# Recurrent gate products in two row halves, and the last chunks one round later

## What is computed

```python
q, k, v, rx, rg, ga, gb = split(modulate(x) @ w_in)      # 16 rounds of two tiles, and v
attn = chunk_band_attention(q, k, v)                     # 8 heads of 64
xc = causal_conv4(rx)
r  = sigmoid(xc_blocks @ wa + ba)                        # 8 blocks of 64 x 64
ig = sigmoid(xc_blocks @ wx + bx)                        # 8 blocks of 64 x 64
a  = exp(-8 * r * softplus(-lam))
u  = sqrt(1 - a*a) * (ig * xc)
h  = linear_scan(h[t] = a[t] * h[t-1] + u[t])
rnn = h * gelu(rg)
x  = x + gate * ((sigmoid(ga) * (attn @ wA) + sigmoid(gb) * (rnn @ wB)) @ w_out)
x  = x + gate * conv_ffn(modulate(x))
y  = rmsnorm(x)
```

## Time and profile before

| what | value |
|---|---|
| time, median of 3 runs | 2693.74 us (2689.85 to 2702.45) |
| span of the profiled execution | 2692.3 us |
| TensorE busy | 2645.6 us, 98% |
| VectorE, ScalarE, GpSimd busy | 1750.8, 1362.9, 628.2 us |
| mean granted TensorE clock | 0.992 |
| DMA | 423.07 MB, mean 157 GB/s |

### The profile page before, as it was taken

The page is one execution under the profiler, slowest core; times in us unless marked ns, Lnnn a source line. Parts: engine busy times, 40 slices in busy tenths (PEclk is TensorE's granted clock), DMA queues, the critical chain, the costliest instruction groups (busy, mean ns, idle before and its releaser), DMA issues.

```text
span 2692.3 us, 50625 instructions
## 1 busy us (share of the span) xinstructions
PE 2645.6 (98%) x18664; PEld 1771.5 (66%) x18664; DVE 1750.8 (65%) x3367; ACT 1362.9 (51%) x2666; POOL 628.2 (23%) x698
## 2 busy tenths in 40 slices
PE   7999999999999999999999999999999999999998
PEld 2466666666668888557996666666666666666665
DVE  4966464655646666776778788888888875242433
ACT  4967474755656666113556555565555653121211
POOL 2600000000008889000000254433344311101000
PEclk9999999999999999999999999999999999999999
DMA  8621322031294442556552354445545438567572
GB/s 281 200 74 66 135 78 105 25 109 71 93 231 95 112 156 105 183 210 202 143 142 69 126 181 166 171 168 189 181 159 179 165 120 325 212 233 262 210 249 106
DMA packets 238419, 423.07 MB, mean 157 GB/s; under 512 B 57816, under 2 KB 162776, under 8 KB 230056
## 3 DMA queue, kind: packets, MB, share of 16 engines
q1 hardware_dynamic: 229400, 412.03, 46.1%
q10 hardware_dynamic: 8848, 8.74, 1.0%
HBM read 283.42 MB, written 139.92 MB: 157 GB/s over the span
## 4 chain that ended last, share of the span: by engine, by line
PE 84%; DVE 5%; ACT 4%; DMA 3%; issue 2%; POOL 1%; SPq 0%; DVEq 0%; ACTq 0%; POOLq 0%
PE ps L2988 57%; PE ps L3240 14%; PE ps L3080 4%; PE ps L3067 3%; PE ps L3056 2%; DMA arena<-in_w_mod_rest 2%; PE ps L2912 1%; ACT arena L1600 1%; PE ps L3094 1%; POOL arena L1140 1%; PE ps L3029 1%; DVE arena L2393 1%; DVE arena L2471 1%; ACT arena L1607 1%; DVE arena L2089 0%
## 5 line engine op out<-in xcount | busy, mean ns | idle before, releaser
L2988 PE MATMUL ps<-arena 128*128 128x352 f16 (+1 forms) x11880 | 1613.1, 297 | 5.1 <-ACT arena L1768 2.1
L2988 PEld LDWEIGHTS ps<-arena 128*128 128x128 f16 x11880 | 1100.6, 97 | 513.1 <-ACT arena L1768 2.5
L3240 PE MATMUL ps<-arena 128*128 128x352 f16 x2772 | 414.9, 310 | 0.5 <-DVE arena L2689 0.5
L3240 PEld LDWEIGHTS ps<-arena 128*128 128x128 f16 x2772 | 264.7, 96 | 150.8 <-issue 1.0
L1197 POOL TENSOR_TENSOR arena<-arena 128x128 f32<-128x128 f32 x44 | 30.6, 695 | 740.4 <-DMA arena<-in_w_down 740.1
L3094 PE MATMUL ps<-arena 128*128 128x424 f16 (+1 forms) x960 | 172.5, 341 | 2.1 <-DVE arena L2471 1.4
L1760 ACT ACTIVATE arena<-ps 128x352 f32<-128x352 f32 x264 | 116.3, 460 | 98.8 <-PE ps L2988 98.8
L1153 POOL CAST arena<-arena 64x512 f16<-64x512 f32 x8 | 4.9, 610 | 689.6 <-DMA arena<-in_cache_kT 689.3
L3080 PE MATMUL ps<-arena 128*128 128x64 f32 (+2 forms) x1200 | 151.0, 272 | 0.5 <-DVE arena L2435 0.5
L1207 POOL TENSOR_TENSOR arena<-arena 128x176 f32<-128x176 f32 (+1 forms) x57 | 56.2, 986 | 398.4 <-DMA arena<-ffn_hidden 398.4
L3080 PEld LDWEIGHTS ps<-arena 128*128 128x128 f32 (+2 forms) x1200 | 144.4, 193 | 3.4 <-issue 2.1
(11 more groups left out here) (239 smaller groups left out, 3587.1 us busy)
## 6 DMA issues: line engine op xcount, KB each, us to landing
hidden_combinations<-arena SPq DMA_DIRECT2D x48, 616.0 KB, 3.2
arena<-hidden_combinations SPq DMA_DIRECT2D x24, 1232.0 KB, 7.8
arena<-in_w_up SPq DMA_DIRECT2D x44, 512.0 KB, 4.9
down_combinations<-arena SPq DMA_DIRECT2D x44, 448.0 KB, 2.8
ffn_hidden<-arena SPq DMA_DIRECT2D x44, 440.0 KB, 3.1
arena<-down_combinations SPq DMA_DIRECT2D x10, 1792.0 KB, 7.8
arena<-down_combinations SPq DMA_DIRECT2D x20, 896.0 KB, 6.9
arena<-ffn_hidden SPq DMA_DIRECT2D x50, 352.0 KB, 3.9
```

Of the source, the lines that this page charges most:

```text
L2988: mm = pe.matmul(out, wt[:, k, wp, :], act_t[:, k, hp], start=(first and k == 0 and n == 0), stop=(last and k == K - 1 and n == 2), skip_g ...
L3240: mm = pe.matmul(ps[:, down_bank(n, k), 0:CF].rearrange("p (w t) -> p w t", w=2), dwt(i)[:, wi, wp, :], dact[i][:, :, bi, hp, :], start=(i ...
```

## The change

1. Gate products in two row halves. The weights of a group shrink from 2 x 128 to 128 columns: rows 0 to 63 hold block 2j of both gates, rows 64 to 127 block 2j + 1 of both, with the gates' columns swapped. A chunk has six matmuls again, but each of 64 rows, alternating between the row halves and between banks 4 and 5. Each bank then holds both gates of one block. Both tanh of gates are halved by partition, and two of the four read one partition half and write the other.
2. gates(j, s) is cut in two: gates (the four tanh) and decays (tanh and exp). In i = 0 a c21 is put between them.
3. Chunk 4 gets its gate product in i = 2 behind c = 2 (was i = 1 behind c = 6), chunk 5 in i = 2 behind c = 4 (was c = 2). The steps of chunks 3 to 5 on ScalarE and VectorE move later accordingly; those of chunk 5 end in round i = 3, and with them q_hi and q_lo (from the end of i = 2), k_hi (behind the first copies) and k_lo (behind p_block(r, 0)).
4. VectorE makes the split of weights 2 of the next round (proj_lo) in i = 2 behind the scan of chunk 4.
5. The sync queue stores gate row 0 of the last round ahead of the weight loads instead of behind them. The recurrent stores keep their places.

```diff
-        gw, gws = bufT[:, 0:2 * P], at_(51560, 4 * P, F16).rearrange("p (s n) -> p s n", s=2)
+        gw, gws = bufT[:, 0:P], at_(51560, 2 * P, F16).rearrange("p (s n) -> p s n", s=2)
...
-            return NS * j + (0, 2, 5, 6)[i]
+            return NS * j + (0, 2, 4, 6)[i]
...
             for r in range(NR):
                 j, i = r // 4, r % 4
+                if r and kind_of(r - 1) == GATES:
+                    gate_row(r - 1, 0)
                 if r + 1 < NR:
                     round_tiles(r + 1)
...
                 if r and kind_of(r - 1) == GATES:
-                    gate_row(r - 1, 0)
                     gate_row(r - 1, 1)
...
             def gates(j, s):
...
-                act.activation(cols, ps[:, 4, 0:w], ACT.Tanh, scale=0.5 * CS, bias=half_bias(0, j)).then_inc(x_act, 1)
-                act.wait_ge(x_gate, 2 * n + 2)
+                act.activation(cols[low], ps[low, 4, 0:w], ACT.Tanh, scale=0.5 * CS, bias=half_bias(0, j)[low])
+                act.activation(cols[high], ps[high, 5, 0:w], ACT.Tanh, scale=0.5 * CS, bias=half_bias(0, j)[high])\
+                    .then_inc(x_act, 1)
                 keep_above_zero(act, x_d2, 3 * (n - 1))
-                act.activation(bufI[s % 2][:, 0:w], ps[:, 5, 0:w], ACT.Tanh, scale=0.5 * CS, bias=half_bias(1, j)).then_inc(x_act, 1)
+                act.activation(bufI[s % 2][low, 0:w], ps[high, 4, 0:w], ACT.Tanh, scale=0.5 * CS,
+                               bias=half_bias(1, j)[high])
+                act.activation(bufI[s % 2][high, 0:w], ps[low, 5, 0:w], ACT.Tanh, scale=0.5 * CS,
+                               bias=half_bias(1, j)[low]).then_inc(x_act, 1)
+
+            def decays(j, s):
...
# ScalarE, the loop over r
-                    for q in range(2 if i == 2 else 0, 3):
+                    for q in range((0, 1, 2, 0)[i], 3):
                         c21(r - 1, q)
-                    if i == 2:
-                        rnn_hi(j, 3)
...
                 if i == 2:
-                    gates(j, 4)
+                    chunk_hi(j, 4)
+                    root(j, 3)
+                    rnn_hi(j, 3)
                 if i == 3:
-                    k_hi(j)
+                    root(j, 5)
+                    q_hi(j)
                 for q in range(3):
                     copy(r, 0, q)
...
                 if i == 2:
-                    root(j, 4)
                     tap(j, 5)
-                    chunk_hi(j, 5)
-                    rnn_hi(j, 4)
+                if i == 3:
+                    k_hi(j)
+                    rnn_hi(j, 5)
...
# VectorE, the loop over r
                 if i == 2:
-                    recur1(j, 4)
-                    recur2(j, 4)
-                    conv(j, 5)
+                    chunk_lo(j, 4)
+                    recur2(j, 3)
+                    rnn_product(j, 3)
+                    rnn_lo(j, 3)
+                if i == 3:
+                    recur2(j, 5)
+                    rnn_product(j, 5)
+                    q_lo(j)
+                for q in range(3):
+                    p_block(r, 0, q)
                 if i == 3:
                     k_lo(j)
-                for q in range(3):
-                    p_block(r, 0, q)
+                    rnn_lo(j, 5)
...
                 if i == 2:
-                    rnn_lo(j, 5)
+                    recur1(j, 5)
...
# TensorE
-                for g in range(2):
-                    for m, (wp, hp) in enumerate(PASSES):
-                        mm = pe.matmul(ps[:, 4 + g, 0:w], gws[:, wp, P * g:P * g + P], xsp[hp][:, 0:w],
+                for m, (wp, hp) in enumerate(PASSES):
+                    for g in range(2):
+                        own = slice(64 * g, 64 * g + 64)
+                        mm = pe.matmul(ps[:, 4 + g, 0:w], gws[own, wp, :], xsp[hp][own, 0:w],
                                        start=(m == 0), stop=(m == 2))
-                    mm.then_inc(x_gate, 1)
-
-            GATE_SLOTS = {(0, 3): 0, (0, 5): 1, (1, 2): 2, (1, 4): 3, (1, 6): 4, (2, 2): 5}
+                        if m == 2:
+                            mm.then_inc(x_gate, 1)
+
+            GATE_SLOTS = {(0, 3): 0, (0, 5): 1, (1, 2): 2, (1, 4): 3, (2, 2): 4, (2, 4): 5}
```

More of the change, by code:

```diff
@@ L750, in _ @@
                         sp.wait_ge(x_d2, 3 * NS * j)
-                    sp.dma_start(gw, a["w_rgate"][j].rearrange("p g m -> p (g m)")).then_inc(gw_loaded, 16)
+                    sp.dma_start(gw, a["w_rgate"][j]).then_inc(gw_loaded, 16)
                 if r and kind_of(r - 1) == GATES:
-                    gate_row(r - 1, 0)
                     gate_row(r - 1, 1)
@@ L1478, in gates @@
                 n, (t0, w) = NS * j + s, chunk(s)
-                act.wait_ge(x_gate, 2 * n + 1)
+                low, high = slice(0, 64), slice(64, 128)
+                act.wait_ge(x_gate, 2 * n + 2)
                 act.wait_ge(x_conv, 3 * n + 3)
                 cols = rowA[:, t0:t0 + w]
-                act.activation(cols, ps[:, 4, 0:w], ACT.Tanh, scale=0.5 * CS, bias=half_bias(0, j)).then_inc(x_act, 1)
-                act.wait_ge(x_gate, 2 * n + 2)
+                act.activation(cols[low], ps[low, 4, 0:w], ACT.Tanh, scale=0.5 * CS, bias=half_bias(0, j)[low])
+                act.activation(cols[high], ps[high, 5, 0:w], ACT.Tanh, scale=0.5 * CS, bias=half_bias(0, j)[high])\
+                    .then_inc(x_act, 1)
                 keep_above_zero(act, x_d2, 3 * (n - 1))
-                act.activation(bufI[s % 2][:, 0:w], ps[:, 5, 0:w], ACT.Tanh, scale=0.5 * CS, bias=half_bias(1, j)).then_inc(x_act, 1)
+                act.activation(bufI[s % 2][low, 0:w], ps[high, 4, 0:w], ACT.Tanh, scale=0.5 * CS,
[3 more added lines that the diff above has]
+            def decays(j, s):
+                n, (t0, w) = NS * j + s, chunk(s)
+                cols = rowA[:, t0:t0 + w]
                 act.wait_ge(x_act, 4 * n + 1)
@@ L1546, in _ @@
                     gates(j, 2)
+                    decays(j, 2)
                     tap(j, 3)
                 if i == 2:
-                    gates(j, 5)
+                    chunk_hi(j, 5)
+                    gates(j, 4)
+                    decays(j, 4)
                 if r + 1 < NR:
@@ L1556, in _ @@
                     chunk_hi(j, 3)
+                if i == 2:
+                    root(j, 4)
                 for q in range(3):
@@ L1562, in _ @@
                     gates(j, 0)
+                    decays(j, 0)
                     chunk_hi(j, 1)
@@ L1566, in _ @@
                 if i == 2:
-                    root(j, 5)
+                    rnn_hi(j, 4)
                 if r + 1 < NR:
@@ L1576, in _ @@
                     gates(j, 3)
+                    decays(j, 3)
                     tap(j, 4)
                 if i == 2:
-                    rnn_hi(j, 5)
+                    gates(j, 5)
+                    decays(j, 5)
                 if r + 1 < NR:
@@ L1583, in _ @@
                     gates(j, 1)
-                if i == 1:
-                    root(j, 3)
-                    chunk_hi(j, 4)
+                    c21(r, 0)
+                    decays(j, 1)
                 if i == 1:
@@ L2331, in _ @@
                 if i == 2:
-                    chunk_lo(j, 5)
-                    rnn_product(j, 4)
-                    rnn_lo(j, 4)
+                    conv(j, 5)
                 if i == 0:
@@ L2345, in _ @@
                 if i == 2:
-                    recur1(j, 5)
+                    chunk_lo(j, 5)
+                    recur1(j, 4)
                 if r + 1 < NR:
                     for c in range(3):
+                        if c == 2 and i == 2:
+                            recur2(j, 4)
+                            rnn_product(j, 4)
                         proj_lo(r + 1, c)
@@ L2357, in _ @@
                     rnn_product(j, 2)
-                if i == 2:
-                    recur2(j, 5)
-                    rnn_product(j, 5)
                 if r + 1 < NR:
+                    if i == 2:
+                        rnn_lo(j, 4)
                     proj_lo(r + 1, 3)
@@ L2380, in _ @@
                     recur1(j, 1)
-                if i == 1:
-                    recur2(j, 3)
-                    rnn_product(j, 3)
-                    rnn_lo(j, 3)
-                if i == 2:
-                    q_lo(j)
             def ada_tile(n):
@@ L3021, in gate_products @@
                 n, (t0, w) = NS * j + s, chunk(s)
-                r = 4 * j + (0, 0, 1, 1, 1, 2)[s]
+                r = 4 * j + (0, 0, 1, 1, 2, 2)[s]
                 pe.wait_ge(gw_lo, 2 + j + 1)
@@ L3291, in lay_out @@
            cols(i["norm_ffn_g"][0]), cols(i["rnn_conv_w"][0]), cols(i["rnn_conv_b"][0]), cols(i["rnn_gate_a_b"][0]),
-           cols(i["rnn_gate_x_b"][0]), cols(i["rnn_lambda"][0]), cols(i["state_rnn_h"][0, 0]),
+           np.roll(cols(i["rnn_gate_x_b"][0]), 64, axis=0), cols(i["rnn_lambda"][0]), cols(i["state_rnn_h"][0, 0]),
            cols(i["state_rnn_conv"][0, 0]), cols(i["ffn_conv_w"][0]), cols(i["ffn_conv_b"][0]),
@@ L3298, in lay_out @@
```

(6 more changed lines are left out.)

6 lines of the change are left out of this document (1 added, 5 removed).

## The result

The changed kernel takes 2703.8 us (median of 9 runs, 2700.3 to 2707.0), the kernel before took 2694.6 us in the same session (9 runs, 2689.8 to 2702.5). The ratio is 1.0036 with a 95% interval of 1.0025 to 1.0047: slower by about a third of a per cent, within what the prediction calls no change, inside its range, and 8 us above its centre. The profiled spans say the same, 2701.7 against 2692.3 us.

What follows compares the result with a forecast made beforehand. The prediction took TensorE's back-to-back matmul stream as the bound, with little spare time at attention's start. Row halves -3.4, ScalarE and VectorE 0, attention's loads +5.9 gave +2.5 us on 2693.7: 2696 us, range 2686 to 2706.

Steps and rivals of the forecast that it cites:

- What bounds the kernel: Projection stage: only the number of back-to-back TensorE matmuls counts; attention's start has 4.4 us of spare time.
- The pair of halves: Gate blocks: two 64-row matmuls run at once, three slots of 0.15 us; with the row switch 3.4 us saved in all.
- rival (b): Gate blocks: halves run one after the other, +7.4 us, with the loads +13.3 us, 2707 us; chance 0.12.
- The switch: Gate blocks: going from 128 to 64 rows and back costs 0.18 + 0.13, together 0.31 us a block.
- ScalarE at nothing: Projection stage: four half tanh add 0.9 to 1.1 us of ScalarE a chunk but cost 0, bound 2 us.
- its own sign: Prediction wrong if the stage shortens by over 8 us, attention's idle time is missing, or a projection product waits for a copy.
- the sum for the start of round i = 2: ScalarE's steps from the last p_block through the first copy: 10.2 us, due at 10.74, 0.5 us to spare.
- Rival (c): Start of rounds i = 2: late copy or gate chunk opens 1 us gaps in four groups, 2700 us; within the forecast's 0.60.
- The sync queue: Round 15: late recurrent store delays attention's loads by 10.5 us, to 752.5; cost +5.9 us, bounds 0 and 10.5.
- its 1.0 for the clock: Start of attention: 1.0 us added for a lower granted clock behind the wait for the values.
- The sum: Whole kernel: -3.4 (row halves) + 0 (ScalarE, VectorE) + 5.9 (loads of attention) = +2.5 us, 2696 us.
- The rest of part 3 at nothing: Sync queue: earlier gate row 0, halved gate weights and the late store in rounds 3, 7 and 11 cost 0.

Runs made afterwards that it cites:

- e5: Changed kernel with gate products over 128 rows and two tanh as before, leaving the new order alone: 2700.9 us, 1.0021 of the kernel before.
- e2: Changed kernel with the tanh of gate row 0 of rounds i = 1 moved behind the last c21 and two splits: 2696.5 us, 1.0012 of the kernel before.
- e1: Changed kernel with round 15's last head rows and recurrent store behind attention's loads, in rounds 3, 7, 11 that store behind the key row: 1.0012 of the kernel before.
- e6: Changed kernel with attention's loads first, middle tanh later, and gate matmuls three of one half, then three of the other: 1.0009 of the kernel before.
- e7: The kernel before, unchanged, measured and profiled once more: 1.0001 of the kernel before.

## Why the prediction was right or wrong

- **What bounds the kernel: right.** The stage's matmul stream and the start of attention hold 8.5 to 9.0 us of the difference of 9.3.
- **The pair of halves: right in kind.** The pairs start together, and rival (b) is out. **The switch was mis-sized:** I took 0.31 us from weight loads of small fp32 transposes; it is 0.09 us going in (0.24 against 0.149), and coming out 0.56 - 3 x 0.16 = 0.08. Together 0.17, about half. So a block gives 0.24 us, not 0.14, and the term is -5.8 and not -3.4. The page TensorEngine Tiling (Array Packing) of the Trainium skill, Tiling Modes, Key Properties, says that a change of mode drains the engine; the trace agrees that each side costs something, and puts it at 0.09 and 0.08 us.
- **ScalarE at nothing: wrong, and this is the step that failed.** By its own sign, a projection product that waits for a copy, the prediction is wrong here. Two errors. The four tanh start 0.56 to 0.58 us apart where full ones start 0.45 apart (371.13 and 371.58 in e5), so a chunk costs 1.4 us more and not 0.9 to 1.1. And the sum for the start of round i = 2 began with "p_block comes at about 0.3 us into the round". It ends at 381.24, which is 2.3 us into it: VectorE gets the gates' results later, runs the convolution of chunk 4 and a split (377.46 to 379.88) first, and only then the p_block. (The 0.3 doesn't follow from the prediction's own rows either: a tanh that starts 1.37 us ahead of the round, put off by 0.9 in a round 1.2 us shorter, gives 0.7.) With the true start the sum of 10.2 us against 10.74 would have been 12.2, late by 1.5. The rest of that sum was right: 9.9 us from the tanh through the first copy, and TensorE goes on 10.2 us behind the tanh (381.28 to 391.47). I also looked for the loss at the first copy alone; the larger part (1.31 of 1.81 us) fell on c21, queued behind the waiting tanh, which the sum doesn't have. Rival (c) was this mechanism, at 1 us a group in place of 1.8. I gave it no chance of its own but counted it into the forecast. e5 (no waits with two tanh and full rows) and e2 (nearly none with the one tanh moved) show it.
- **The sync queue: right in kind, the size a little low.** 752.5 was forecast for the first load and 752.59 measured, but so close by chance: the stage ends 1.0 us later than before, and from its end the first load comes 9.7 us later, not 10.5. In exchange the loads take 22.5 us from the first issue to the last in place of 21.1, and the last, issued at 775.05, lands 4.8 us later, at 779.8, where 778.2 was forecast. TensorE waits for keys, for VectorE and for the values, 4.1 + 1.6 + 1.6 us. The first product with the values is 6.8 us late, where the forecast without its 1.0 for the clock is 4.9; the hundredth is 7.4 late, so the clock cost 0.6. Together 7.4 against 5.9. e1 and e5 each show it alone. The clock behind it did fall, at 0.50 until 779.8 and 0.81 for the 10 us after:

```profile
773.90:779.80 5.90, 2.46 (x10) 0.97 (x10) 1.65 (x13) 1.92 (x8) 0.00 (x0) 0.50 1.15 312
779.80:790.00 10.20, 9.90 (x58) 7.22 (x59) 5.83 (x30) 6.40 (x19) 4.67 (x7) 0.81 0.87 333
```

- **The sum.** Forecast -3.4 + 0 + 5.9 = +2.5; measured -5.8 + 7.2 + 7.4 = +8.8, with medians 9.3 apart. The missed 7.2 us is rival (c) and outweighs the 2.4 by which I had the row halves too dear. That 2703.8 lies in the range of 2686 to 2706 is in part luck: the two errors have opposite signs, and it lies above the 2691 to 2701 that the forecast had with (c) in it, nearest to the 2707 of rival (b), whose mechanism isn't there.
- **The rest of part 3 at nothing: right.** Gate row 0 ahead of the weight loads, the smaller gate weights and the late store in rounds 3, 7 and 11 open no gap (e5: 623.18 us, no idle time).

## What to carry to other kernels

When work on an engine off the path grows, don't compare its busy share with the stage; follow the chain that the longest wait on that engine stands in, with the true end of the step it waits for, and name every copy queued behind it. An instruction that may wait goes behind those that free a bank for TensorE: moving one tanh was worth 5.8 us. And a store whose source became later is a stop for everything behind it in its queue, in a mend as much as in the change: here the late recurrent store held attention's loads, and the key rows moved behind these loads held the gate row. For a wait that names no releaser, add each transfer's time to landing to its issue and see which sum the wait ends with.

## What the runs showed of the hardware that I had not expected

- Six fp16 matmuls of 64 rows in two row halves take 0.56 us to the next product whether they alternate or come as three and three (changed kernel and e6); in both they start in pairs, so in e6 not in the order of the program. The switch from 128 to 64 rows costs 0.09 us in such a stream.
- A tanh over 64 partitions and 353 columns lasts 0.55 us like one over 128, but the next one starts 0.56 to 0.58 us later and not 0.45: the overlap of neighbours is lost. The Trainium skill (ScalarE: Activation LUTs, What ACT_TABLE_LOAD costs) has back-to-back ACTIVATEs overlap by about 93 ns; the full ones here overlap by 0.11 us, the half ones by -0.01 to -0.03. What takes it away (reading two banks, the offset between the partitions read and written, or the half width) was not tried.
- With an unchanged program the granted clock falls at different places in different executions; between stage and merge the same kernel took 5.5 us longer in the execution with two more such falls (e7). Right behind the projection stage it fell in eleven of the 14 profiled executions, not in e6 or in the two of the kernel before, and that cost 0.3 to 1.1 us by the first nine products with the values.
